# Expert blocks of a mixture of experts: token rows fetched by an indirect transfer and turned, in place of products with a matrix of zeros and ones

## The chip, the cores and the metric

The kernel runs on one core of one Trainium2 chip. The metric is the device time of one execution in microseconds (us), as the median over runs.

## What is computed

The program is three layers of a model on 512 tokens of width 1024, in float32: two layers of attention, convolution and pooling mixers with cross-attention and an MLP, and a third with four more mixers and a mixture of 32 experts, each token going to 4 of them. Only that last part, `moe_ffn`, is touched:

```python
logits = (xt @ router_w + router_b).astype(jnp.float32)
top_logits, top_idx = lax.top_k(logits, TOP_K)            # 4 of 32 experts
gates = jax.nn.softmax(top_logits, axis=-1)
...
def run_block(args):                                       # one block: up to 128 tokens of one expert
    tok, e = args
    hmid = xt[tok] @ w_gu[e] + b_gu[e]                     # xt[tok]: the gather
    glu = jnp.minimum(hmid[:, 0::2], SWIGLU_LIMIT)
    lin = jnp.clip(hmid[:, 1::2], -SWIGLU_LIMIT, SWIGLU_LIMIT)
    act = glu * jax.nn.sigmoid(SWIGLU_ALPHA * glu) * (lin + 1.0)
    return act @ w_down[e] + b_down[e]
```

`xt` is the RMS-normalised activation times a gain. The up product is 1024 x 2048, the down product 1024 x 1024.

## The kernel before

`out_norm_and_route` makes the last residual, normalises it tile by tile (128 tokens each), turns it for the router, and computes for every token and expert the place that the token has among the expert's tokens (`T.place`). It also keeps the normalised rows `T.y` as two float32r parts, `high` and `low` (`Parts.round` on ACT, L88, and `Parts.rest` on DVE, L91), 4 tiles of 128 tokens by 1024 features.

`first_blocks` then runs the 32 experts j = 0..31 in order, four to a turn of a hardware loop (experts 0 to 3 ahead of the loop, 28 to 31 behind it). Each expert's weights are 6 units of 2 MB (0 to 3 up, 4 and 5 down) in a ring of 6 slots of SBUF (`ring_view`). SP loads unit n of expert j+1 as soon as expert j is done with slot n, so the ring holds one expert.

An expert with at most 64 tokens is a half expert: `up_half`, `turn_act_half`, `down_half` use plain float32 products on 64 columns of the array, two at a time. One with more is a full expert. Its first unit is used in plain float32 (`up_parted`, L3829); for units 1 to 5, ACT rounds each quarter of the unit into the one buffer `moe_w_high` (L88), DVE takes the rest (L91), and `unit_products` makes three float32r products of each pair of quarter and half bank (L3799, L3800, L3804). DVE also makes the gated activation (`clip` L3856 and L3857, `multiply` L3863 and L3868) and splits its turned form (`split_act`, L3873). An expert ends with the bias products of the down part (L3820 full, L3660 half; those of the up part are L3820 and L3633).

The gather is two products. `make_sel` (DVE, L3513) writes for a pair of experts a matrix of zeros and ones, 512 tokens by 2 x 128 places; `gather` (PE, L3594 and L3595) multiplies the two parts of `T.y` by it. Every expert step of PE has two calls of it for the following pair, one between the up products and the turning of the activation, one between that turning (L3812, L3640) and the last down products; each call is 16 products of 256 columns. `save_gather` (DVE, L3530) multiplies the result by the gain into `T.xg`, which lies in the space of `hT`.

An expert with more than 128 tokens has its further tokens in an extra block; `extra_blocks` runs these behind the 32, here two, both half. They use the same `gather`, with nothing else around it. `combine_and_finish` fetches the 4 rows of each token with indirect transfers (POOL, L4578) and sums them.

Of the kernel before, what the change touches and what calls it, by code (L numbers as in the profile page):

```python
# [14 lines left out]
P = 128  # L15
# [90 lines left out]
class Core:  # L106


    def __init__(self, nc, ctx, ins, out):
# [15 lines left out]
        self.rows = nc.dram_tensor("expert_rows", [BLOCKS, P, D], F32, kind="Internal").ap()  # L125
        self.x_rows = nc.dram_tensor("x_rows", [P, TT, D], F32, kind="Internal").ap()
# [565 lines left out]
class TileNorm:  # L692

# [5 lines left out]
    def __init__(self, k, ctx, gain, dst, first=()):  # L701
        self.k = k
        self.tiles = list(first) + [(k.x[:, t, :], dst[:, :, t * P:(t + 1) * P], gain) for t in range(TT)]
        self.y = k.sb("tile_y", [P, 2, D], ctx=ctx)
        self.ss = k.sb("tile_ss", [P, len(self.tiles)], ctx=ctx)
        self.rms = k.sb("tile_rms", [P, len(self.tiles)], ctx=ctx)
        self.rstd = k.sb("tile_rstd", [P, len(self.tiles)], ctx=ctx)

    def square_and_root(self, act, t, added):
        k = self.k  # L710
        if added is not None:
            act.wait_ge(k.bank_free.sem, added)
        if t >= 2:
            act.wait_ge(k.turned.sem, k.turned.at(2 * t - 2))
        act.activation(self.y[:, t % 2, :], self.tiles[t][0], ACT.Square, accum_out=self.ss[:, t:t + 1])\
# [5 lines left out]
    def scale(self, dve, t):  # L721
        k = self.k
        dve.wait_ge(k.roots.sem, k.roots.at(t + 1))
        dve.reciprocal(self.rstd[:, t:t + 1], self.rms[:, t:t + 1]).then_inc(k.rstd.sem, 1)
        dve.wait_ge(k.rstd.sem, k.rstd.at(t + 1))
        dve.tensor_scalar(self.y[:, t % 2, :], self.tiles[t][0], self.rstd[:, t:t + 1], None, ALU.mult)\
           .then_inc(k.normalised.sem, 1)

    def turn(self, pe, t):
# [5 lines left out]
        for g in range(2):  # L735
            for c in range(4):
                f = 4 * g + c
                ins = pe.transpose(k.psum[:, self.TURNED + g, c * P:(c + 1) * P], self.y[:, t % 2, f * P:(f + 1) * P],
# [3 lines left out]
    def save_even(self, dve, t):  # L742
        k = self.k
        dve.wait_ge(k.turned.sem, k.turned.at(2 * t + 1))
        _, dst, gain = self.tiles[t]
        dve.tensor_tensor(dst[:, 0:4, :], k.psum[:, self.TURNED, :].rearrange("p (c s) -> p c s", c=4),
                          gain[:, 0:4].unsqueeze(2).broadcast_to([P, 4, P]), ALU.mult)\
           .then_inc(k.turned_even.sem, 1)

    def save_odd(self, act, t):  # L750
        k = self.k
        act.wait_ge(k.turned.sem, k.turned.at(2 * t + 2))
        _, dst, gain = self.tiles[t]
        for c in range(4):
            ins = act.activation(dst[:, 4 + c, :], k.psum[:, self.TURNED + 1, c * P:(c + 1) * P], ACT.Copy,
                                 scale=gain[:, 4 + c:5 + c])
        ins.then_inc(k.turned_odd.sem, 1)

    def passed(self):
        k = self.k  # L760
        for signal in (k.squares, k.roots, k.rstd, k.normalised, k.turned_even, k.turned_odd):
            signal.passed(len(self.tiles))
        k.turned.passed(2 * len(self.tiles))
# [2714 lines left out]
class Experts:  # L3478


    def __init__(self, k, name, tables, one_by_one):
# [7 lines left out]
        self.sel_ready = signal("sel_ready")  # L3489
        self.gathered = signal("gathered")  # L3490
# [15 lines left out]
    def make_sel(self, dve, r, blocks=2):  # L3506

        T = self.tables
        if not self.one_by_one and self.waits_from(r, 1):
            dve.wait_ge(self.gathered, 4 * r)  # L3510
        for h in range(blocks):
            for t in range(TT):
                ins = dve.tensor_scalar(T.sel[:, t, h, :], T.iota[:, :], T.place[:, t, bass.ds(blocks * r + h, 1)], None,  # L3513
                                        ALU.is_equal)
        ins.then_inc(self.sel_ready, 1)

# [6 lines left out]
    def save_gather(self, dve, n, half, par):  # L3523

        k, T = self.k, self.tables
        for b in range(2):
            dve.wait_ge(self.gathered, 2 * n + b + 1)
            f = 4 * half + 2 * b
            gain = T.gain[:, f:f + 2].unsqueeze(2).broadcast_to([P, 2, 2 * P])
            dve.tensor_tensor(T.xg[:, par, f:f + 2, :], k.psum[:, b, :].rearrange("p (f s) -> p f s", f=2),  # L3530
# [1123 lines left out]
```

## Time and profile before

| what | value |
|---|---|
| time, median of 3 runs | 3115.11 us (3108.37 to 3116.99) |
| time of the profiled execution | 3102.57 us |
| its span, first to last instruction | 3100.8 us |
| granted TensorE clock, mean over the span | 0.946 |
| PE busy | 2814.6 us, 91% |
| DVE busy | 1620.0 us, 52% |
| ACT busy | 1053.1 us, 34% |
| POOL busy | 154.8 us, 5% |
| HBM read and written | 581.73 MB and 41.16 MB |

The span is the time from the first to the last instruction. A clock of 1.00 is 2.4 GHz, 0.50 is 1.2 GHz. PE is TensorE's matmuls, PEld its weight loads, DVE VectorE, ACT ScalarE, POOL GpSimd, SP the engine that issues the weight loads from HBM. Busy times of matmuls are modelled and overlap, so distances between starts are used below and not sums of durations.

### The profile page before, as it was taken

The page shows a single profiled execution, that of the slowest core. Times are in us where ns is not written, and L with a number is a line of the kernel's source. Part 1 is how long each engine was busy: PE and PEld are TensorE (multiplying, and loading weights), DVE is VectorE, ACT ScalarE, POOL GpSimd, SP SyncE. Part 2 cuts the span into 40 slices and gives each one's busy share as a digit, 9 for nine tenths or more (in the row PEclk, how much of TensorE's full clock was granted, in tenths as well). Part 3 has the DMA queues.
Part 4 walks back from the last instruction along what each step waited for, and adds up shares of the span by engine and source line. Part 5 has one row for each costly group of instructions (what it writes and reads, how often), then busy time and mean ns, then how long its engine had stood idle before and what let it go on. Part 6 is the DMA issues. An engine that isn't in the chain of part 4 may idle for free. (4 is left out here: it accounts for less than half of the span.)

```text
span 3100.8 us, 36680 instructions
## 1 busy us (share of the span) xinstructions
PE 2814.6 (91%) x13802; PEld 2044.2 (66%) x13803; DVE 1620.0 (52%) x2423; ACT 1053.1 (34%) x1468; POOL 154.8 (5%) x171
## 2 busy tenths in 40 slices
PE   7877989999999899999966878999999999899982
PEld 6655768888878688888754665654766565466541
DVE  4864554444555544446855546652855454266413
ACT  4444443232224432233332241330634233144301
POOL 0530000000000000000012020000000000000002
PEclk9988999999999999999987788999999999999986
DMA  3110315444323132222210037999999899999994
GB/s 131 58 51 28 109 61 189 175 166 170 118 103 116 62 116 82 108 88 78 95 55 1 1 123 274 387 409 408 388 361 372 338 409 369 409 374 347 409 385 152
DMA packets 186386, 626.00 MB, mean 202 GB/s; under 512 B 9747, under 2 KB 15538, under 8 KB 185810
## 3 DMA queue, kind: packets, MB, share of 16 engines
q1 hardware_dynamic: 173328, 577.51, 49.1%
q10 hardware_dynamic: 10530, 37.02, 3.0%
q0 software_dynamic: 2304, 8.39, 0.7%
q8 instruction: 153, 2.51, 0.3%
q14 instruction: 71, 0.58, 0.1%
HBM read 581.73 MB, written 41.16 MB: 201 GB/s over the span
## 5 line engine op out<-in xcount | busy, mean ns | idle before, releaser
L91 DVE TENSOR_TENSOR unit_low<-unit_whole,unit_high 128x4096 fp32r<-128x4096 f32 (+3 forms) x95 | 287.3, 3029 | 177.4 <-ACT unit_high L88 165.5
L667 PE MATMUL psum<-tokens_high,unit_high 128*128 128x512 f32 (+2 forms) x1016 | 372.1, 366 | 4.4 <-PEq L873 1.6
L667 PE MATMUL psum<-tokens_high,unit_low 128*128 128x512 f32 (+2 forms) x1016 | 368.3, 363 | 0.0
L667 PE MATMUL psum<-tokens_low,unit_high 128*128 128x512 f32 (+2 forms) x1016 | 368.3, 362 | 0.0
L88 ACT ACTIVATE unit_high<-unit_whole 128x4096 fp32r<-128x4096 f32 (+2 forms) x65 | 225.8, 3474 | 377.1 <-PE psum L667 286.5
L88 ACT ACTIVATE moe_w_high<-ring_slot 128x1024 fp32r<-128x1024 f32 x208 | 215.9, 1056 | 60.0 <-PE psum L3804 59.1
L3627 PE MATMUL psum<-ring_slot,hT 128*64 128x512 f32 x1008 | 226.8, 599 | 7.5 <-DMA ring_slot<-in_moe_w_gu 7.5
L667 PEld LDWEIGHTS psum<-tokens_high,unit_high 128*128 128x128 f32 (+1 forms) x1016 | 190.9, 188 | 38.0 <-DVE unit_low L91 4.0
L667 PEld LDWEIGHTS psum<-tokens_low,unit_high 128*128 128x128 f32 (+1 forms) x1016 | 190.9, 188 | 31.6 <-issue 1.6
L667 PEld LDWEIGHTS psum<-tokens_high,unit_low 128*128 128x128 f32 (+1 forms) x1016 | 190.9, 188 | 30.6 <-issue 0.2
L667 PE MATMUL psum<-unit_high,hidden_high 128*128 128x512 f32 x512 | 199.5, 390 | 0.0
L667 PE MATMUL psum<-unit_high,hidden_low 128*128 128x512 f32 x512 | 199.2, 389 | 0.0
L667 PE MATMUL psum<-unit_low,hidden_high 128*128 128x512 f32 x512 | 199.2, 389 | 0.0
L3670 DVE TENSOR_SCALAR moe_glu<-psum 128x256 f32<-128x256 f32 x42 | 17.8, 425 | 330.9 <-PE psum L3633 239.8
L3627 PEld LDWEIGHTS psum<-ring_slot,hT 128*64 128x64 f32 x1008 | 76.8, 138 | 147.3 <-issue 146.2
L3594 PE MATMUL psum<-moe_sel,moe_y_high 128*128 128x256 f32 x576 | 151.9, 301 | 10.2 <-DVE moe_sel L3513 7.9
L1155 DVE TENSOR_TENSOR x_residual<-psum,x_residual 128x512 f32<-128x512 f32 x128 | 84.4, 687 | 117.7 <-PE psum L667 117.7
L3595 PE MATMUL psum<-moe_sel,moe_y_low 128*128 128x256 f32 x576 | 144.4, 288 | 0.0
L3799 PE MATMUL psum<-moe_w_high,moe_xg_high 128*128 128x512 f32 x312 | 131.1, 420 | 0.0
L91 DVE TENSOR_TENSOR unit_high<-ring_slot,moe_w_high 128x1024 fp32r<-128x1024 f32 x104 | 122.8, 1220 | 15.4 <-ACT moe_w_high L88 15.0
L3594 PEld LDWEIGHTS psum<-moe_sel,moe_y_high 128*128 128x128 f32 x576 | 113.3, 197 | 24.9 <-issue 14.2
L3684 ACT ACTIVATE moe_sig<-moe_glu 128x256 f32<-128x256 f32 x42 | 17.5, 417 | 313.5 <-DVE moe_glu L3670 313.4
(642 smaller groups left out, 5351.8 us busy)
## 6 DMA issues: line engine op xcount, KB each, us to landing
ring_slot<-in_moe_w_gu SPq DMA_DIRECT2D x102, 2048.0 KB, 16.0
unit_whole<-in_moe_w_gu SPq DMA_DIRECT2D x34, 2048.0 KB, 12.9
ring_slot<-in_moe_w_down SPq DMA_DIRECT2D x34, 2048.0 KB, 12.3
ring_last_slot<-in_moe_w_down SPq DMA_DIRECT2D x34, 2048.0 KB, 15.7
unit_whole<-in_w_up SPq DMA_DIRECT2D x16, 2048.0 KB, 8.4
unit_whole<-in_w_down SPq DMA_DIRECT2D x16, 2048.0 KB, 7.6
expert_rows<-zero_row ACTq DMA_DIRECT2D x15, 1536.0 KB, 5.3
unit_whole<-in_w_in SPq DMA_DIRECT2D x5, 2048.0 KB, 7.7
```

The source lines that it names most:

```text
L88: return act.activation(self.high, self.whole, ACT.Copy)
L91: return dve.tensor_tensor(self.low, self.whole, self.high.bitcast(F32), ALU.subtract)
L667: ins = pe.matmul(bank, a, c, start=(first and m == 0), stop=(last and m == len(parts) - 1))
L1155: dve.tensor_tensor(x, bank, x, ALU.add).then_inc(k.bank_free.sem, 1)
L3594: pe.matmul(bank, T.y.high[:, t, features], chosen, start=(t == 0), stop=False)
L3595: ins = pe.matmul(bank, T.y.low[:, t, features], chosen, start=False, stop=(t == TT - 1))
L3627: ins = pe.matmul(banks[g], xg[:, c, 0:HALF], w[c // HALF_K][:, c % HALF_K, g * 512:(g + 1) * 512], start=(c == 0), stop=False)
L3670: dve.tensor_scalar(T.glu[:, pair, :], bank[:, :, 0], 7.0, None, ALU.min).then_inc(self.glu_ready, 2)
L3684: act.activation(T.sig[:, pair, :], T.glu[:, pair, :], ACT.Sigmoid, scale=1.702).then_inc(self.gate_ready, 2)
L3799: pe.matmul(banks[g], a.high[:, f, :], w.high[:, cols], start=(first and q == 0), stop=False)
```

## The change

The normalised rows stay whole (`T.y`, float32) and are also stored to a table in HBM, `y_rows`, one DMA of 512 KB per tile, issued by ACT in place of the rounding. For every expert, `make_sel` writes the matrix of zeros and ones for this expert alone in bfloat16, and `find_tokens` multiplies it by a table `T.token` of two columns, which gives each place its token number (in two parts). `save_tokens` adds the parts up to an integer index; a place without a token gets an index beyond the table, which the transfer skips. `fetch_rows` is an indirect DMA by POOL of up to 128 rows of 4 KB into one of two buffers `T.y_of`; `turn_rows` turns them with 4 transposes per half, and `save_gather` applies the gain. The extra blocks still gather with a product, now in plain float32 on 128 columns.

```diff
-    def make_sel(self, dve, r, blocks=2):
+    def make_sel(self, dve, j, par):
+        if self.waits_from(j, 2):
+            dve.wait_ge(self.index_full, j - 1)
+        for t in range(TT):
+            ins = dve.tensor_scalar(T.sel[:, par, t, :], T.iota[:, :], T.place[:, t, bass.ds(j, 1)], None, ALU.is_equal)
         ins.then_inc(self.sel_ready, 1)
+    def find_tokens(self, pe, j, par):
+        pe.wait_ge(self.sel_ready, j + 1)
+        if self.waits_from(j, 2):
+            pe.wait_ge(self.xg_ready, 2 * (j - 1))
...
+        for t in range(TT):
+            ins = pe.matmul(k.psum[:, 1, 0:2], T.sel[:, par, t, :], T.token[:, t, :], start=(t == 0), stop=(t == TT - 1))
+        ins.then_inc(self.index_full, 1)
+    def save_tokens(self, dve, j):
+        dve.wait_ge(self.index_full, j + 1)
+        dve.tensor_scalar(T.index[:, bass.ds(j, 1)], k.psum[:, 1, 0:1], k.psum[:, 1, 1:2], float(S), ALU.add, ALU.add)\
+           .then_inc(self.index_ready, 1)
+    def fetch_rows(self, pool, j):
+        pool.wait_ge(self.index_ready, j + 1)
+        if j >= 2:
+            pool.wait_ge(self.gathered, 2 * (j - 2) + 2)
+        pool.indirect_dma_start(T.y_of[:, j % 2, :], None, k.y_rows, bass.IndirectOffsetOnAxis(ap=T.index[:, j:j + 1], axis=0),
+                                bounds_check=S - 1, oob_is_err=False).then_inc(self.fetched[j % 2], 16)
+    def turn_rows(self, pe, j, half, par, fetches=None, saved=None):
+        if half == 0:
+            pe.wait_ge(self.fetched[par], 16 * fetches)
...
+        else:
+            pe.wait_ge(self.index_ready, saved)
...
+        for f in range(4):
+            ins = pe.transpose(k.psum[:, half, f * P:(f + 1) * P], T.y_of[:, par, (4 * half + f) * P:(4 * half + f + 1) * P],
+                               k.ident[:, :])
+        ins.then_inc(self.gathered, 1)
...
# first_blocks, PE, one expert step
-                if ahead:
-                    E.gather(pe, pair + 1, j + 2, h, 0, saved=2 * (j + 1) + 1)
+                if following:
+                    if not (last and b == PER_ROUND - 2):
+                        E.find_tokens(pe, j + 2, par)
+                    E.turn_rows(pe, j + 1, 0, 1 - par, (PER_ROUND // 2) * i + (b + 1) // 2 + 1)
...
-                if ahead:
-                    E.gather(pe, pair + 1, j + 2, h, 1, saved=2 * (j + 1) + 2)
+                if following:
+                    E.turn_rows(pe, j + 1, 1, 1 - par, saved=j + 3 if not (last and b == PER_ROUND - 2) else EXPERTS)
# first_blocks, DVE, behind the activation of expert j
-                    E.save_gather(dve, j + 2, b % 2, 1 - b // 2)
+                        E.save_tokens(dve, j + 2)
+                    E.save_gather(dve, j + 1, 0, 1 - par)
+                    E.save_gather(dve, j + 1, 1, 1 - par)
# out_norm_and_route, ACT
-                    y_parts(t).round(act).then_inc(y_rounded, 1)
+                    act.dma_start(k.y_rows[t * P:(t + 1) * P, :], T.y[:, t, :]).then_inc(T.y_stored, 16)
```

TensorE in the step of a full expert, from its last down products of unit 4 on, before. `moe_act` is the activation that is turned, and its two parts are `moe_actT_high` and `moe_actT_low`:

```order
L3804 MATMUL psum<-moe_w_high,moe_actT_low 128x512 x2
L3812 MATMUL psum<-ident,moe_act 128x128 [waits first_act_ready]
L3812 MATMUL psum<-ident,moe_act 128x128 x3
L4145 UNCONDITIONAL_BRANCH
L3594 MATMUL psum<-moe_sel,moe_y_high 128x256 [waits first_xg_ready]
L3595 MATMUL psum<-moe_sel,moe_y_low 128x256
```

Fourteen more such products follow there. The same place of the changed kernel (`hT` holds the fetched rows):

```order
L3849 MATMUL psum<-ident,moe_act 128x128 [waits first_act_ready]
L3849 MATMUL psum<-ident,moe_act 128x128 x3
L4192 UNCONDITIONAL_BRANCH
L3556 MATMUL psum<-ident,hT 128x128 [waits first_xg_ready,first_index_ready]
L3556 MATMUL psum<-ident,hT 128x128 x3
```

Sixteen products give way to four transposes, and the wait is for `index_ready` of this step too. VectorE at the end of the same step, before:

```order
L91 TENSOR_TENSOR moe_last_low<-ring_last_slot,moe_w_high 128x1024 [waits unit_rounded] x4
L3873 TENSOR_TENSOR moe_actT_low<-psum,moe_actT_high 128x512 [waits first_actT_ready]
L4176 UNCONDITIONAL_BRANCH
L3530 TENSOR_TENSOR hT<-psum,feature_vectors 128x2x256 [waits first_gathered] x2
L3520 COPY moe_bias_ones<-moe_bias_pick 128x128
```

And in the changed kernel, where L3910 is the split of the turned activation that was L3873:

```order
L3910 TENSOR_TENSOR moe_actT_low<-psum,moe_actT_high 128x512 [waits first_actT_ready]
L4225 UNCONDITIONAL_BRANCH
L3532 TENSOR_SCALAR moe_index<-psum 128x1 [waits first_index_full]
L3571 TENSOR_TENSOR hT<-psum,feature_vectors 128x512 [waits first_gathered] x2
L3563 COPY moe_bias_ones<-moe_bias_pick 128x128
```

The write of the index, for which PE's second group of transposes waits, stands behind the split of the turned activation.

## Rows read from the trace of the kernel before

**Rows 1.** Windows: engines' busy us (instructions), granted clock, DMA share, GB/s.

```profile
1950.40:2971.80 1021.40, 986.66 (x4650) 587.34 (x4648) 519.95 (x777) 373.48 (x455) 0.00 (x0) 0.98 0.98 384
1950.40:2143.40 193.00, 187.45 (x918) 106.96 (x917) 93.94 (x172) 62.27 (x80) 0.00 (x0) 1.00 1.01 400
2605.80:2696.50 90.70, 81.82 (x415) 35.79 (x414) 17.36 (x52) 9.04 (x20) 0.00 (x0) 0.96 1.00 394
```

**Rows 2.** Groups of instructions, 1850 to 3101 us: busy us, mean ns, idle before.

```profile
L3594 PE MATMUL psum<-moe_sel,moe_y_high 128*128 128x256 f32 x576 | 151.9, 301 | 10.2 <-DVE moe_sel L3513 7.9 <-ACT moe_o L3704 2.3
```

**Rows 3.** Timeline of PE, expert 14 (full): start us, us, engine, line.

```profile
2353.50 7.13 PE L3829 MATMUL psum<-unit_whole,hT 128*128 128x512 f32 x16
...
2378.18 0.60 PE L3820 MATMUL psum<-moe_bias_parts,moe_bias_ones 128*128 128x512 bf16 x2
...
2380.52 0.39 PE L3799 MATMUL psum<-moe_w_high,moe_actT_high 128*128 128x512 f32 x1
...
2386.10 0.60 PE L3812 MATMUL psum<-ident,moe_act 128*128 128x128 f32 x4
2386.45 0.36 PE L3594 MATMUL psum<-moe_sel,moe_y_high 128*128 128x256 f32 x1
...
2388.41 0.40 PE L3799 MATMUL psum<-moe_w_high,moe_actT_high 128*128 128x512 f32 x1
...
2394.47 1.88 PE L3829 MATMUL psum<-unit_whole,hT 128*128 128x512 f32 x4
```

**Rows 4.** Timeline of PE, expert 30 (full, without gather products), idle before in brackets.

```profile
2924.54 0.60 PE L3820 MATMUL psum<-moe_bias_parts,moe_bias_ones 128*128 128x512 bf16 x2
...
2934.74 0.73 PE L3804 MATMUL psum<-moe_w_high,moe_actT_low 128*128 128x512 f32 x2 [1.18 <-DVE moe_actT_low L3873]
...
2940.06 1.51 PE L3627 MATMUL psum<-unit_whole,hT 128*64 128x512 f32 x6
```

**Rows 5.** Timeline of DVE, expert 30.

```profile
2929.47 4.62 DVE L91 TENSOR_TENSOR moe_last_low<-ring_last_slot,moe_w_high 128x1024 fp32r<-128x1024 f32 x4
2934.01 0.68 DVE L3873 TENSOR_TENSOR moe_actT_low<-psum,moe_actT_high 128x512 fp32r<-128x512 f32 x1
```

**Rows 6.** Timeline of PE, half experts: expert 13, then the second extra block.

```profile
2341.26 0.39 PE L3633 MATMUL psum<-moe_bias_parts,moe_bias_ones 128*64 128x512 bf16 x2
...
2343.80 0.66 PE L3640 MATMUL psum<-ident,moe_act 128*128 128x128 f32 x4
...
2346.27 3.65 PE L3655 MATMUL psum<-ring_slot,moe_actT 128*64 128x512 f32 x16
...
3035.43 0.41 PE L3633 MATMUL psum<-moe_bias_parts,moe_bias_ones 128*64 128x512 bf16 x2
3037.97 0.66 PE L3640 MATMUL psum<-ident,moe_act 128*128 128x128 f32 x4 [2.13 <-DVE moe_act L3677]
3039.38 5.04 PE L3655 MATMUL psum<-ring_slot,moe_actT 128*64 128x512 f32 x16 [0.75 <-ACT moe_actT L3695]
```

**Rows 7.** Waits and granted clock: PE's timeline at experts 7 and 12, three windows.

```profile
2120.86 4.51 PE L3627 MATMUL psum<-ring_slot,hT 128*64 128x512 f32 x20 [1.71 <-DMA ring_slot<-in_moe_w_gu]
2284.60 2.07 PE L3829 MATMUL psum<-unit_whole,hT 128*128 128x512 f32 x2 [3.28 <-issue]
...
2110.00:2125.00 15.00, 13.29 (x66) 4.71 (x64) 1.61 (x4) 1.60 (x3) 0.00 (x0) 1.00 1.03 410
2284.60:2327.30 42.70, 42.70 (x184) 31.00 (x184) 31.99 (x34) 24.18 (x26) 0.00 (x0) 0.96 0.93 359
3036.00:3044.00 8.00, 5.28 (x20) 1.98 (x22) 1.55 (x4) 1.07 (x3) 0.00 (x0) 0.79 0.00 0
```

**Rows 8.** PE's first up product; a fill and the last indirect transfers (POOL).

```profile
1887.56 2.80 PE L3627 MATMUL psum<-unit_whole,hT 128*64 128x512 f32 x12 [0.78 <-DVE hT L3530]
1794.11 1.80 POOL L4367 MEMSET moe_up_bias<- 128x2048 f32 x1 [45.49 <-POOLq L378]
ring_slot<-expert_rows,moe_row POOLq DMA_INDIRECT x12, 6.3
```

More of the change, by code:

```diff
@@ L125, in __init__ @@
         self.rows = nc.dram_tensor("expert_rows", [BLOCKS, P, D], F32, kind="Internal").ap()
+        self.y_rows = nc.dram_tensor("y_rows", [S, D], F32, kind="Internal").ap()
         self.x_rows = nc.dram_tensor("x_rows", [P, TT, D], F32, kind="Internal").ap()
@@ L689, in early_banks, with __init__ @@
         yield b
-class TileNorm:
+class RouterNorm:
     TURNED = 6
[L701 to L707, printed above, removed]
+    def __init__(self, k, ctx, gain, y):
+        self.k, self.gain, self.y = k, gain, y
+        self.ss = k.sb("tile_ss", [P, TT], ctx=ctx)
+        self.rms = k.sb("tile_rms", [P, TT], ctx=ctx)
+        self.rstd = k.sb("tile_rstd", [P, TT], ctx=ctx)
     def square_and_root(self, act, t, added):
         k = self.k
[L711 to L715, printed above, removed]
+        act.wait_ge(k.bank_free.sem, added)
+        act.activation(self.y[:, t, :], k.x[:, t, :], ACT.Square, accum_out=self.ss[:, t:t + 1])\
            .then_inc(k.squares.sem, 1)
@@ L3489, in __init__ @@
         self.sel_ready = signal("sel_ready")
+        self.index_full = signal("index_full")
+        self.index_ready = signal("index_ready")
+        self.fetched = [signal(f"rows_fetched{r}") for r in range(2)]
         self.gathered = signal("gathered")
@@ new lines, in make_extra_sel @@
+    def make_extra_sel(self, dve, b):
+        T = self.tables
+        for t in range(TT):
+            ins = dve.tensor_scalar(T.sel_whole[:, t, :], T.iota[:, :], T.place[:, t, bass.ds(b, 1)], None, ALU.is_equal)
+        ins.then_inc(self.sel_ready, 1)
+    def find_tokens(self, pe, j, par):
+        k, T = self.k, self.tables
+        pe.wait_ge(self.sel_ready, j + 1)
+        if self.waits_from(j, 2):
+            pe.wait_ge(self.xg_ready, 2 * (j - 1))
+        elif j == 1:
+            pe.wait_ge(self.index_ready, 1)
+        for t in range(TT):
+            ins = pe.matmul(k.psum[:, 1, 0:2], T.sel[:, par, t, :], T.token[:, t, :], start=(t == 0), stop=(t == TT - 1))
+        ins.then_inc(self.index_full, 1)
@@ L4123, in is_half, with _ @@
             return eng.value_load(T.count[0:1, bass.ds(j, 1)], min_val=0, max_val=S) < HALF + 1
+        @block.gpsimd
+        def _(pool):
+            pool.memset(T.y_of, 0.0).then_inc(k.pool_made.sem, 1)
+            pool.wait_ge(k.pool_made.sem, k.pool_made.at(1))
+            pool.wait_ge(T.y_stored, 16 * TT)
+            for j in range(EXPERTS):
+                E.fetch_rows(pool, j)
         @block.tensor
@@ L4168, in step @@
             def step(i, b, j, first, last):
+                par = b % 2
                 parted = not (first and b == 0)
-                xg = T.xg[:, b // 2, :, (b % 2) * P:(b % 2 + 1) * P]
+                xg = T.xg[:, par]
+                following = not (last and b == PER_ROUND - 1)
                 with dve.If(is_half(dve, j)):
```

188 lines of the change are left out of this document (90 added, 98 removed).

## The prediction

> **What bounds the kernel now.** I read the windows first. From the start of expert 2 to the end of expert 31 [rows 1] PE is busy 986.66 of 1021.40 us and the DMA engines have a share of 0.98 at 384 GB/s, with 400 and 394 GB/s in two stretches inside. So two resources are near their limit at once: where PE is freed, a transfer can take over. The other engines are at half. Next the groups [rows 2]: the first of the two gather products is 151.9 us busy in 576 instructions, and as many of the second follow them one by one. That is not what they cost, since matmuls overlap. So the timeline, at one full expert and one half.
>
> Expert 14, full [rows 3], takes 2353.50 to 2394.47 = 41.0 us and PE never waits. The first gather call lies between the up bias (2378.18) and the down products of unit 4 (2380.52): 2.34 us with the 0.26 us of the bias, so 2.08. The second lies between the transposes of the activation (2386.10) and unit 5 (2388.41): 2.31 us, of which 0.35 are the transposes, so 1.96. The gather costs 4.0 us per expert, 0.12 us per product.
>
> Now the last experts, which in the kernel before have no gather products at all, as there is no expert left to gather for. Expert 30 is full [rows 4]: from its up bias at 2924.54 to the next expert at 2940.06 it takes 15.52 us, where expert 14 takes 16.29 from the same bias. Four us of products are gone and 0.8 us is gained. The rest has turned into waits, and the rows say for whom: the product L3804 at 2934.74 waited for DVE L3873, the split of the turned activation, and DVE was busy without a pause ahead of it [rows 5]: four splits of unit 5 from 2929.47, then L3873 from 2934.01. From the up bias on, DVE needs 10.2 us until PE can go on (2934.74 - 2924.54), whatever PE does in the meantime. A full expert's gather is cover over DVE.
>
> The half expert tells the same [rows 6]. In expert 13 the transposes of the activation start 2.54 us behind the up bias (2341.26, 2343.80) with a gather call in between, and in an extra block, with nothing in between, also 2.54 us behind it (3035.43, 3037.97), PE idle for 2.13. The activation sets that time. Only the second distance shrinks: 2.47 us to the down products with a gather call (2343.80, 2346.27), 1.41 without (3037.97, 3039.38). So a half expert gains 1.06 us, not 4.0. And the down products behind this idle time took 5.04 us for 16, against 3.65 in expert 13: the granted clock of 3036 to 3044 is 0.79 [rows 7], between full speed and 0.5, where expert 13 ran at full speed.
>
> **The change, part by part.** *Half experts.* `find_tokens` and four transposes stand in the first gap and four transposes in the second. They are shorter than the idle time there: four transposes start 0.35 us apart as a group [rows 3], and the four products with two columns I put at 0.3 in all (bounds: nothing, and four of the 0.12 us of a gather product). So 2.13 becomes about 1.4 us of idle time and 0.75 about 0.45. Does the clock fall? At 2120.86 PE had been idle for 1.71 us and the clock stayed at 1.00 [rows 7]; behind 2.13 and 0.75 it fell. I take no fall, hence -1.06 us; with a fall it is +0.33 (5.04 - 3.65 = 1.39).
>
> *Full experts.* The second group of transposes waits for `index_ready` of this step (`saved=j+3`), because `find_tokens` has used the same PSUM bank; DVE writes that index only behind L3873, as the order shows. Queued behind this wait on PE are all products of unit 5. From the up bias: DVE's split is seen by PE at 10.2 us [rows 4]. The index is one more small DVE instruction, 0.2 (bounds 0.1 and 0.4): 10.4. Transposes 0.36: 10.76. Unit 5 and its bias, from 2388.41 to 2394.47 [rows 3], 6.06: 16.82. Before: 16.29. So **+0.53 us**, although 4.0 us of products are removed. `find_tokens` and the first transposes, ahead of unit 4, cost nothing as DVE covers them: without them PE would wait the longer. PE's idle time is then one piece: unit 4 ends near 6.5 us, the transposes of the activation near 7.1, the wait until 10.4: 3.3 us. Such a piece is in the trace. At the turns of the loop PE is idle 3.28 us, and expert 12 behind it takes 42.70 us at a mean clock of 0.96 [rows 7], where expert 14 took 41.0: the fall costs 1.7. I take it for every full expert: 0.53 + 1.7 = **+2.2 us**; expert 30, which gets transposes now, 16.82 + 1.7 - 15.52 = +3.0.
>
> For the transposes the Trainium skill has another price ("TensorE: Matmul & The Clock Gate", Part 4: PE-mode transpose): about 275 ns each in a kernel's context. The row says 0.35 us for four, in float32. By the page each full expert would be 0.75 us longer and the sum 10 us greater; the sum here goes by the row.
>
> *The transfers.* A fetch of expert j+1 is issued when its index is written, in the step of expert j-1, and needed behind the up products of expert j, over 20 us later even for two half experts. The last indirect transfers land 6.3 us after issue [rows 8]. Hidden. But they add bytes: 2048 rows of 4 KB at most, 8.4 MB or 64 rows per expert, 0.66 us each at the 400 GB/s of the busier stretch [rows 1]. Where PE waits for weights that counts in full, and there PE's gains and losses are swallowed.
>
> *The rest.* POOL's small fills and the table stand where POOL then waits for ACT. The stores of `y_rows` replace ACT's rounding, and DVE's four splits fall away, on a stretch in which PE's order of router and count products ends last; I count 0. At the start, two matrices, a product, the fill of `T.y_of` (1.80 us for 2048 columns [rows 8]) and a fetch of 6.3 us or more beside 4 MB of other loads stand in place of the gather; PE's first up product was at 1887.56 and I expect it within -2 and +4 us of that. I take 0. The Trainium skill has a lower price for such a fetch ("DMA: Bandwidth & Descriptors", Anatomy of one DMA — SWDGE (gpsimd) path: 2.0 us and the bytes at 436 GB/s, so 3.2 us for 512 KB). By it the start would be 3 us earlier, and the total by as much; the row is for the same kind of transfer and I stay with it. The gather of an extra block was 64 products of 0.12 us and becomes 32 in float32, which the trace counts as two each; with the 0.09 us of a float32 transpose per piece as the lower bound and 0.15 as the upper, -2 to +2 us each. I take 0.
>
> **The sum.** Of the experts 2 to 29, 12 are full and 16 half. Experts 2 to 8 (five half, two full) run at 400 GB/s and end on waits for weights, experts 21 to 23 (all half) at 394 [rows 1]. There only the bytes count: 10 x 0.66 = +6.6. Outside: 10 full x 2.2 = +22, 8 half x -1.06 = -8.5, expert 30 +3.0. Together **+23 us**. The profiled execution takes 3102.57 us, so 3126. It lies 12.5 below the median of the runs shown, 3115.11, to which the same step gives **3138**. A difference under 0.3%, 9 us, can't be told from none here.
>
> **The rivals.**
> *The half experts lose the clock too.* Their idle time shrinks only from 2.9 to about 1.9 us in two pieces, and the extra block shows the fall. Then the 8 outside the stretches that wait for weights pay 1.39 us each, and up to 8 inside them as well: 11 to 22 us more, 3149 to 3160. Chance 0.13.
> *The wait costs less than it seems, no change.* If the clock does not fall behind most of the waits of 3.3 us, as it did not behind 1.71, or the fall runs out before unit 5 starts, full experts come out at 0 to +0.5 and the sum at -1 to +5 (expert 30 at +1), 3114 to 3120. Chance 0.22.
> *Faster: what PE is freed of does come out.* This needs DVE's index in time: if the split of the turned activation is done when the transposes of the activation are, because PE hands on the rounding buffer earlier. Then a full expert saves 4.0 less 1.0 of new products and transposes and a half 1.06: -30 - 8.5 + 6.6 = -32, 3083. It decides from the point where DVE needs under 7 us from the up bias; it needed 9.5 until L3873 started in expert 30. Chance 0.11.
> *A fetch is late.* If the indirect transfers, beside loads that keep the engines full, take over 20 us, PE waits in every half step: if it is 25 us, 5 us in each of 16 half steps: +80, 3218. The 6.3 us of the last transfers [rows 8] speak against it, though fewer loads ran beside them. Chance 0.04.
> The forecast itself has 0.50.
>
> **How the numbers follow.** The forecast's own range, with the start (-2 to +4), the index (0.1 to 0.4 us each) and the extra blocks (4 us either way), is 3125 to 3150. Eight in ten must take in most of no change and of the slower case: 3105 to 3160. Faster by over 0.3% is the third rival and a tail of the second: 0.13. No change 0.22. Slower: 0.65.
>
> **What would show it.** In the changed trace, a full expert away from the loop's turn takes about 43 us, with one wait of some 3.3 us of the transposes L3556 for DVE's index L3532, and a granted clock of 0.5 in the products of unit 5. A half expert takes 25.1 us. The mean clock of the expert stage falls from 0.98 to about 0.93. Wrong would be: full experts of 38 us (DVE is no bound), clock at 1.00 behind the waits, or PE waiting for `rows_fetched`.

## The result and the profile after

The changed kernel takes 3120.11 us, median of 20 runs (3111.32 to 3130.64), the kernel before beside it 3109.60 us, median of 20 (3096.18 to 3120.75): a ratio of 1.0032, 95% interval 1.0020 to 1.0044. In a second measurement it was 3120.39 against 3107.06 us, 1.0051 (1.0037 to 1.0065). So the change costs 0.3 to 0.5% by the ratios, 10 to 16 us. Its profiled execution took 3119.28 us with a span of 3117.2 us and a mean granted clock of 0.936.

The windows of the changed kernel, with the columns of [rows 1]: from the start of expert 2 to the end of expert 31, then experts 2 to 8 and 21 to 23.

```profile
1948.50:2990.80 1042.30, 924.76 (x4060) 528.54 (x4097) 524.34 (x815) 371.71 (x455) 27.68 (x28) 0.97 0.98 384
1948.50:2180.40 231.90, 203.04 (x910) 104.85 (x914) 100.04 (x195) 63.44 (x84) 6.92 (x7) 0.96 1.01 400
2619.20:2709.10 89.90, 74.82 (x355) 29.34 (x354) 16.96 (x51) 9.02 (x20) 2.97 (x3) 0.94 1.01 397
```

Against [rows 1] PE has 62 us less to do in the experts (986.66 to 924.76), and they take 20.9 us longer (1021.40 to 1042.30). The groups of instructions from 1850 us on, as in [rows 2], say what PE waited for ahead of its new transposes (the number behind the last bar is the idle time, then its releasers):

```profile
L3556 PE MATMUL psum<-ident,hT 128*128 128x128 f32 x256 | 42.3, 291 | 51.3 <-DVE moe_index L3532 40.7 <-DMA hT<-y_rows,moe_index 10.4
```

151.9 us of products of one of two lines gave way to 42.3 us, and 40.7 us of waiting for the index came with them. The timeline of PE in expert 14, the expert of [rows 3], its start and then from the last bias product of the up part on:

```profile
2364.69 0.70 PE L3866 MATMUL psum<-unit_whole,hT 128*128 128x512 f32 x1
...
2389.29 0.38 PE L3857 MATMUL psum<-moe_bias_parts,moe_bias_ones 128*128 128x512 bf16 x1
2389.51 0.24 PE L3525 MATMUL psum<-moe_token,moe_sel 128*128 128x2 bf16 x4
2389.61 0.64 PE L3556 MATMUL psum<-ident,hT 128*128 128x128 f32 x4
2390.00 0.47 PE L3836 MATMUL psum<-moe_w_high,moe_actT_high 128*128 128x512 f32 x1
...
2395.68 0.60 PE L3849 MATMUL psum<-ident,moe_act 128*128 128x128 f32 x4
2399.64 0.66 PE L3556 MATMUL psum<-ident,hT 128*128 128x128 f32 x4 [3.36 <-DVE moe_index L3532]
2400.20 0.79 PE L3836 MATMUL psum<-moe_w_high,moe_actT_high 128*128 128x512 f32 x1
...
2403.72 0.40 PE L3836 MATMUL psum<-moe_w_high,moe_actT_high 128*128 128x512 f32 x1
...
2407.86 2.31 PE L3866 MATMUL psum<-unit_whole,hT 128*128 128x512 f32 x5
```

PE is idle for 3.36 us at the second group of transposes, and the products behind it are spaced 0.43 and not 0.23 us until 2403.6. From 2364.69 to 2407.86 the expert takes 43.2 us, where it took 41.0. The timeline of DVE there answers to [rows 5]:

```profile
2394.23 4.62 DVE L91 TENSOR_TENSOR moe_last_low<-ring_last_slot,moe_w_high 128x1024 fp32r<-128x1024 f32 x4
2398.77 0.69 DVE L3910 TENSOR_TENSOR moe_actT_low<-psum,moe_actT_high 128x512 fp32r<-128x512 f32 x1
2399.37 0.21 DVE L3532 TENSOR_SCALAR moe_index<-psum 128x1 f32 x1
```

The index stands behind five splits, and PE starts when it is written. Three windows, the wait, the 3.4 us behind it, and the same products in expert 10, with the clock as the third number from the end:

```profile
2396.30:2399.64 3.34, 0.00 (x1) 0.00 (x1) 3.34 (x6) 1.12 (x2) 0.00 (x0) 1.00 1.02 408
2400.20:2403.60 3.40, 3.40 (x9) 2.75 (x9) 1.68 (x6) 0.00 (x0) 0.99 (x1) 0.50 1.03 410
2258.60:2265.00 6.40, 6.33 (x29) 4.79 (x29) 2.06 (x7) 0.00 (x0) 0.99 (x1) 1.00 0.75 299
```

In expert 14 the granted clock is 0.50 for 3.4 us, in expert 10 it stays at 1.00 though its wait is as long. Expert 10 takes 41.6 us. The half expert 13, on PE (compare [rows 6]):

```profile
2353.26 0.39 PE L3670 MATMUL psum<-moe_bias_parts,moe_bias_ones 128*64 128x512 bf16 x2
2353.58 0.25 PE L3525 MATMUL psum<-moe_token,moe_sel 128*128 128x2 bf16 x4
2353.69 0.63 PE L3556 MATMUL psum<-ident,hT 128*128 128x128 f32 x4
2355.80 0.66 PE L3677 MATMUL psum<-ident,moe_act 128*128 128x128 f32 x4 [1.48 <-DVE moe_act L3714]
2356.30 0.61 PE L3556 MATMUL psum<-ident,hT 128*128 128x128 f32 x4
2357.46 3.65 PE L3692 MATMUL psum<-ring_slot,moe_actT 128*64 128x512 f32 x16 [0.55 <-ACT moe_actT L3732]
```

Idle for 1.48 and 0.55 us, forecast 1.4 and 0.45, and the down products take 3.65 us, so the clock stays. The only wait for a fetch is that of the first expert:

```profile
1886.35 1.97 PE L3556 MATMUL psum<-ident,hT 128*128 128x128 f32 x8 [10.38 <-DMA hT<-y_rows,moe_index]
1889.10 3.68 PE L3664 MATMUL psum<-unit_whole,hT 128*64 128x512 f32 x8 [0.78 <-DVE hT L3571]
```

The 32 fetches land 5.1 to 9.7 us after their issue, median 7.9. PE's first up product is at 1889.10 against 1887.56 [rows 8].

### The profile page after: what moved, and what is told of

Read it like the earlier page. It is cut to its first block and busy times, and to the rows that moved or that the text cites. A ratio compares the mean times of both kernels' runs of the same rounds, so it can differ in the third digit from the quotient of the medians.

```text
span 3117.2 us, 35590 instructions
## 1 busy us (share of the span) xinstructions
PE 2743.2 (88%) x13119; PEld 1974.0 (63%) x13163; DVE 1615.4 (52%) x2447; ACT 1047.2 (34%) x1464; POOL 190.6 (6%) x213
## 5 line engine op out<-in xcount | busy, mean ns | idle before, releaser
L668 PE MATMUL psum<-tokens_high,unit_high 128*128 128x512 f32 (+2 forms) x1016 | 372.2, 366 | 4.5 <-PEq L864 1.7
L668 PE MATMUL psum<-tokens_high,unit_low 128*128 128x512 f32 (+2 forms) x1016 | 368.4, 363 | 0.0
L668 PE MATMUL psum<-tokens_low,unit_high 128*128 128x512 f32 (+2 forms) x1016 | 368.3, 362 | 0.0
L88 ACT ACTIVATE unit_high<-unit_whole 128x4096 fp32r<-128x4096 f32 (+2 forms) x65 | 225.8, 3474 | 373.1 <-PE psum L668 282.3
L3664 PE MATMUL psum<-ring_slot,hT 128*64 128x512 f32 x1008 | 225.8, 596 | 11.7 <-DMA ring_slot<-in_moe_w_gu 11.7
L668 PEld LDWEIGHTS psum<-tokens_high,unit_high 128*128 128x128 f32 (+1 forms) x1016 | 190.8, 188 | 38.1 <-DVE unit_low L91 4.1
L668 PEld LDWEIGHTS psum<-tokens_low,unit_high 128*128 128x128 f32 (+1 forms) x1016 | 190.9, 188 | 31.6 <-issue 1.6
L668 PEld LDWEIGHTS psum<-tokens_high,unit_low 128*128 128x128 f32 (+1 forms) x1016 | 190.9, 188 | 30.7 <-issue 0.2
L668 PE MATMUL psum<-unit_high,hidden_high 128*128 128x512 f32 x512 | 199.5, 390 | 0.0
L668 PE MATMUL psum<-unit_high,hidden_low 128*128 128x512 f32 x512 | 199.2, 389 | 0.0
L668 PE MATMUL psum<-unit_low,hidden_high 128*128 128x512 f32 x512 | 199.2, 389 | 0.0
L3721 ACT ACTIVATE moe_sig<-moe_glu 128x256 f32<-128x256 f32 x42 | 17.5, 416 | 322.0 <-DVE moe_glu L3707 322.0
L91 DVE TENSOR_TENSOR unit_low<-ring_slot,moe_w_high 128x1024 fp32r<-128x1024 f32 x104 | 121.2, 1217 | 0.0
L1136 DVE SCALAR_TENSOR_TENSOR hT<-psum,hidden_relu 128x512 f32<-128x512 f32 x64 | 43.8, 689 | 147.3 <-ACT hidden_relu L1108 147.3
L668 PEld LDWEIGHTS psum<-unit_high,hidden_low 128*128 128x128 f32 x512 | 96.1, 188 | 19.9
## 6 DMA issues: line engine op xcount, KB each, us to landing
ring_last_slot<-in_moe_w_down SPq DMA_DIRECT2D x34, 2048.0 KB, 17.1
```

Of the source, the lines that this page charges most:

```text
L88: return act.activation(self.high, self.whole, ACT.Copy)
L91: return dve.tensor_tensor(self.low, self.whole, self.high.bitcast(F32), ALU.subtract)
L668: ins = pe.matmul(bank, a, c, start=(first and m == 0), stop=(last and m == len(parts) - 1))
L1136: dve.scalar_tensor_tensor(out=hidden[j % 2].whole[:, b, :], in0=bank, scalar=0.0, in1=relu[:, h % 2, :], op0=ALU.max, op1=ALU.mult)\
L3664: ins = pe.matmul(banks[g], xg[:, c, 0:HALF], w[c // HALF_K][:, c % HALF_K, g * 512:(g + 1) * 512], start=(c == 0), stop=False)
L3721: act.activation(T.sig[:, pair, :], T.glu[:, pair, :], ACT.Sigmoid, scale=1.702).then_inc(self.gate_ready, 2)
```

## The experiments

Each ratio is against the kernel before, run on the same chip in the same measurement, with its 95% interval. A full expert is said to be away from the turns if it does not follow a turn of the hardware loop (that is, not 12, 20 or 24) and does not end at one (15).

**The index written early.** `save_tokens` is moved ahead of the splits of unit 5 in full experts. In half ones it stands where it stood, behind the activation.

```diff
             multiply(pair)
+            if pair == 1 and tokens:
+                self.save_tokens(dve, j + 2)
             for q in range(HALF_K):
                 self.split_quarter(dve, j, n + 1, q)
```

> The changed kernel, but DVE writes the token index of expert j+2 right behind the second product of the gated activation of a full expert, ahead of the splits of unit 5, and not behind the split of the turned activation. Theory A (the loss is the wait for an index queued late on DVE, and the clock that falls behind it): the waits of 3.36 us before L3556 are gone, the 12 full experts with a full set of transposes take about 40.6 us (expert 30 of the kernel before took 40.2) and not 43.2, the clock stays at 1.00 in them, and the time is about 30 us under the changed kernel, some 20 under the one before: ratio to before 0.993 to 0.996. Theory B (the fetch's bytes and the waits for weights set the time): nothing is gained over the changed kernel, ratio 1.002 to 1.004.

Measured: 3099.10 us, 0.9982 (0.9971 to 0.9994), less of a gain than expected. PE in expert 14 of this kernel (its first product is at 2358.0):

```profile
2389.44 0.60 PE L3556 MATMUL psum<-ident,hT 128*128 128x128 f32 x4
2390.96 0.49 PE L3836 MATMUL psum<-moe_w_high,moe_actT_high 128*128 128x512 f32 x1 [0.92 <-ACT moe_actT_high L3945]
...
2392.96 0.73 PE L3841 MATMUL psum<-moe_w_high,moe_actT_low 128*128 128x512 f32 x2 [0.82 <-DVE moe_actT_low L3910]
...
2398.13 1.45 PE L3866 MATMUL psum<-unit_whole,hT 128*128 128x512 f32 x3
```

One wait of 3.36 us has become two of 0.92 and 0.82 us, and the expert takes 40.1 us. So the place of one DVE instruction of 0.22 us is what turned a small gain into a loss. The two waits that are left are of the kind that expert 30 had before [rows 4]. In experts 2, 5, 9 and 18 the clock fell behind them and these took 41.8 to 42.4 us. Much of the rest of the expected gain is missing where PE waits for weights: in this one trace experts 2 to 8 take 228.4 us and 21 to 23 take 92.3, where the kernel before has 222.5 and 89.4 in the mean of three.

**Few gather products, nothing else.** The kernel before, with 2 of the 16 products in each gather call of the expert steps, so that the experts compute on wrong rows. Nothing is fetched.

```diff
-            for t in range(TT):
+            for t in range(tiles):
...
+                if tiles == TT:
+                    pe.matmul(bank, T.y.high[:, t, features], chosen, start=(t == 0), stop=False)
...
-                    E.gather(pe, pair + 1, j + 2, h, 0, saved=2 * (j + 1) + 1)
+                    E.gather(pe, pair + 1, j + 2, h, 0, saved=2 * (j + 1) + 1, tiles=1)
```

> The kernel before, but each gather call of an expert step makes 2 of its 16 products (one token tile, one part), so the experts compute on a part of the tokens. It shows what the removed products were worth: summed by their distance, 14 x 2 x 0.12 = 3.3 us per expert, 105 us in all, if PE's time counted in full: ratio 0.966. Theory A (they cover DVE and ACT): full experts 40.3 us as expert 30, half experts 25.1 us, or 26.5 and more where the clock falls behind the idle time of 1.9 us: -8 to -25 us, ratio 0.992 to 0.998.

Measured: 3106.05 us, 1.0000 (0.9991 to 1.0010), where 0.992 to 0.998 was expected. Seven eighths of the gather's products, some 3.5 us per expert, are gone, and the time is the same. Full experts away from the turns take 40.1 to 40.2 us where the clock stays and 41.5 to 41.9 where it falls, which it does in 6 of 8. The clock also falls in half experts, in 7 of the 8 that lie outside the stretches that wait for weights. Expert 13 takes 28.4 us, where it took 26.2:

```profile
2341.47 0.66 PE L3641 MATMUL psum<-ident,moe_act 128*128 128x128 f32 x4 [1.72 <-DVE moe_act L3678]
2343.12 6.62 PE L3656 MATMUL psum<-ring_slot,moe_actT 128*64 128x512 f32 x16 [0.68 <-ACT moe_actT L3696]
```

PE is idle for 1.72 and 0.68 us here, and in the changed kernel for 1.48 and 0.55, where expert 13 kept the clock in all three executions. So the gather was cover, as the prediction had it, and its removal alone is worth nothing: the 0.9 to 1.0 us that an expert gains where the clock stays go into the falls and into longer idle times at the turns of the loop (4.6 to 4.8 us where 3.2 to 3.4 us were before).

**No rows moved.** Every index lies beyond the table, so the indirect transfer skips all rows. The experts compute on zeros.

```diff
-        dve.tensor_scalar(T.index[:, bass.ds(j, 1)], k.psum[:, 1, 0:1], k.psum[:, 1, 1:2], float(S), ALU.add, ALU.add)\
+        dve.tensor_scalar(T.index[:, bass.ds(j, 1)], k.psum[:, 1, 0:1], k.psum[:, 1, 1:2], float(2 * S), ALU.add, ALU.add)\
```

> The changed kernel, but each index lies beyond the table, so the 32 transfers are issued and move no row; the experts compute on zeros. It takes 8.4 MB of transfers away and nothing else. Prediction's term: the bytes count 0.66 us per expert where PE waits for weights, 10 experts, so about -7 us against the changed kernel, ratio to before 1.001, with experts 2 to 8 shorter by 5 us and 9 to 20 unchanged. If bytes don't matter at all: ratio 1.003. If the fetch costs the weight loads more than its bytes (their landing time went from 16 to 18 us), over 10 us less: ratio below 1.000.

Measured: 3114.87 us, 1.0031 (1.0019 to 1.0043). In the trace experts 2 to 8 take 224.7 us, against 231.9, 228.8 and 231.5 in three executions of the changed kernel. That looks like 6 us for the rows, but the kernel called Both below moves them and takes 224.7 us there too, and the other variants of the changed kernel that move them take 225.8 to 228.6. So a cost of the rows is not shown. In the whole time the ratio was expected at 1.001 and is that of the changed kernel, 1.0032 and 1.0051, within the uncertainty.

**The wait filled with 13 products.** float32r products of 512 columns into a free bank, behind the transposes of the activation in full experts.

```diff
         self.turn_act_pair(pe, j, 1)
+        x = self.tables.xg_parts.high
+        for n in range(FILLERS):
+            pe.matmul(self.k.psum[:, 4, :], x[:, 0, :], x[:, 0:4, :].rearrange("p f s -> p (f s)"), start=True, stop=True)
```

> The changed kernel with 13 products of 512 float32r columns (3.0 us) put on PE behind the transposes of the activation of a full expert, into a bank that is free there; nobody reads them. The wait for the index stays, only it is filled. Theory A (a wait of 3.3 us costs 1.7 us more by the fall of the clock): full experts take 41.6 us and not 43.2 where the clock fell, the 0.5 level is no longer seen in unit 5, and the time is 12 to 16 us under the changed kernel: ratio to before 0.998 to 1.000. Rival (the fall lies in time that DVE would make PE wait for anyway): full experts stay at 43 us, ratio 1.003.

Measured: 3130.95 us, 1.0090 (1.0072 to 1.0108), slower than the changed kernel, where 0.998 to 1.000 was expected. The eight full experts away from the turns do what was expected, 41.6 to 42.5 us at a clock of 1.00. But PE's idle time at the loop's turns, 3.28 us in [rows 7], has grown:

```profile
2295.03 2.92 PE L3866 MATMUL psum<-unit_whole,hT 128*128 128x512 f32 x3 [9.54 <-issue]
```

Three such turns cost 6.2 us more each, 19 us together.

**The same number of products, 16 columns each.** Their work is gone and their number stays.

> The kernel with 13 filling products in the wait of the full experts, with 16 columns each in place of 512: as many instructions at the same place, but little work. PE's idle time at the loop's turns (experts 11 to 12, 19 to 20, 23 to 24) was 3.3 us without fillers, 9.5 us with 13 of 512 columns, and 3.4 us followed by a second one of 0.7 to 1.9 us with three. If it is the number of instructions in the loop's body that counts, it is 9.5 us again here. If it is what PE did ahead of the turn (work that keeps it from running ahead of its instructions), it is 3.3 us. In the full experts the wait for the index stays above 2 us in either case and the clock falls behind it in most of them, so that they take 43 us.

One execution, 3143.19 us, with 3110.84 us for the kernel before beside it. The turn is still long, so the work of the filling products is not what lengthens it. What is left is that they are there, 52 instructions more in a turn of the loop:

```profile
2303.49 2.92 PE L3866 MATMUL psum<-unit_whole,hT 128*128 128x512 f32 x3 [9.23 <-issue]
```

The wait for the index is 2.0 us here, and the full experts away from the turns take 42.8 to 43.6 us with the clock fallen, but for expert 10 with 41.7.

**Three products in the wait.** Plain float32, 0.89 us each.

```diff
         self.turn_act_pair(pe, j, 1)
+        for n in range(3):
+            pe.matmul(self.k.psum[:, 4, :], xg[:, 0, :], xg[:, 0:4, :].rearrange("p f s -> p (f s)"), start=True, stop=True)
```

> The changed kernel with three plain float32 products of 512 columns (0.89 us each, 2.7 us) in the wait of 3.36 us of every full expert, in place of the 13 float32r products of the earlier kernel, so that the code of a loop turn grows by 12 products and not by 52. If the idle time of 9.5 us at the loop's turns came from the length of the code, it is back at 3.3 us here; the clock then stays at 1.00 in the full experts, these take 41.7 us, the 9 falls of 1.6 us are gone (-14 us in the profile, span 3102 to 3106) and the ratio to the kernel before is 0.998 to 1.000. If something else in the filler lengthened the turn (its place in the code), the turns stay at 9.5 us and the ratio is 1.006 to 1.009. If the falls cost less without the profiler than with it, the turns are 3.3 us and the ratio is 1.001 to 1.003.

Measured: 3113.53 us, 1.0026 (1.0014 to 1.0037), where the changed kernel had 1.0051 in the same measurement: 7 us less by the medians, half of what was expected. The eight full experts away from the turns all take 41.6 to 41.8 us, and none has a fall. At the turns the idle time is 3.38 us again, but in experts 12, 20 and 24 a second one follows:

```profile
2289.65 2.41 PE L3866 MATMUL psum<-unit_whole,hT 128*128 128x512 f32 x5 [3.38 <-issue]
2293.96 4.54 PE L3866 MATMUL psum<-unit_whole,hT 128*128 128x512 f32 x6 [1.90 <-issue]
```

**Both.** The index early, and one float32 product of 0.89 us ahead of unit 4's down products.

> The changed kernel with the index written early (as in the earlier kernel, which measured 0.9982 of the kernel before) and one plain float32 product of 512 columns, 0.89 us, ahead of the down products of unit 4 of a full expert, where PE otherwise waits 0.92 us for DVE. It adds no time if it ends within that wait. If the two waits of 0.92 and 0.82 us together are what let the clock fall in 5 of the full experts (1.7 us each), one of them alone does not: full experts 40.1 us at a clock of 1.00, 5 falls gone, -6 to -9 us, ratio 0.995 to 0.997. If the falls come from elsewhere, the ratio stays at 0.998.

Measured: 3097.46 us, 0.9973 (0.9961 to 0.9984), faster than both kernels: 9.6 us by the medians below the one before, at the upper end of the 0.995 to 0.997 that was expected. All eight full experts away from the turns take 40.2 to 40.9 us at a clock of 1.00. PE in expert 14, where one wait is left:

```profile
2386.30 0.60 PE L3556 MATMUL psum<-ident,hT 128*128 128x128 f32 x4
2387.82 0.49 PE L3836 MATMUL psum<-moe_w_high,moe_actT_high 128*128 128x512 f32 x1 [0.92 <-ACT moe_actT_high L3946]
```

The expectation had the place of the waits wrong. PE does not wait ahead of unit 4; the wait of 0.92 us stands ahead of unit 5, for ACT, and is still there. The added product puts unit 4 and all behind it 0.9 us later, and so the second wait, 0.82 us for the split of the turned activation, is used up.

The falls of experts 2, 5, 9 and 18 are gone, and one each in 12 and 24, 9 us together. Against the index alone only 3 us are seen in the ratio, and the two intervals overlap, so that these two kernels are not told apart. In the profile two falls came back elsewhere, in the half experts 16 and 19 (27.0 and 30.9 us, there 25.3 and 28.8), and experts 21 to 23, which wait for weights, took 93.9 us against 92.3.

**Both kernels again.** Each twice more, nothing altered.

> The changed kernel once more, nothing altered, for two questions. Does the granted clock fall behind the same waits? In its first profile it fell in 9 of the 12 full experts from 2 to 27 that have the wait of 3.36 us, and each fall cost 1.6 us. If a fall behind this wait is a matter of phase, other experts are spared this time, the total is 8 to 11 of 12, and the span lies within 5 us of 3117.2. If it is fixed by the work, experts 10, 15 and 18 are spared again. The rival is that the profile of the changed kernel was an unlucky one: then 4 to 6 fall now and the span is 3107 to 3111. Time against the kernel before: 1.002 to 1.004.

> The kernel before once more, one look, for how far two profiled executions of one kernel differ. The first had a span of 3100.8 us with no fall of the granted clock in a full expert away from the loop's turn. If such falls are a matter of phase only where PE is idle, there are none again, a full expert is 41.0 us again, and the span differs by less than 4 us, the difference lying in the stretches that wait for weights. If the first profile was a lucky one by the 12.5 us that it lay below the shown median, the span is 3108 to 3114 now.

> The changed kernel a third time. From the start of expert 2 to the end of expert 31 the two executions so far took 1042.3 and 1036.0 us, with the granted clock falling in 9 of 12 full experts in both, and in the same ones. I expect 1034 to 1044 us and 8 to 10 falls; experts 10, 15 and 18 are spared if it is fixed by what lies ahead of them.

> The kernel before a third time. From the start of expert 2 to the end of expert 31 the two executions so far took 1022.5 and 1022.3 us, while the unchanged code ahead of the experts ended up to 8 us apart. I expect 1021 to 1025 us for the experts, and no fall of the granted clock in a full expert away from the loop's turns.

The windows from the start of expert 2 to the end of 31, first the second and third execution of the changed kernel, then of the one before:

```profile
1948.30:2984.30 1036.00, 926.29 (x4099) 527.17 (x4097) 524.70 (x815) 371.89 (x455) 27.78 (x28) 0.97 0.98 385
1947.90:2992.20 1044.30, 930.44 (x4099) 531.59 (x4097) 523.99 (x815) 371.60 (x455) 27.69 (x28) 0.96 0.98 383
```

```profile
1958.00:2980.30 1022.30, 985.98 (x4651) 586.81 (x4649) 520.91 (x781) 373.48 (x455) 0.00 (x0) 0.98 0.99 384
1955.00:2972.40 1017.40, 980.51 (x4650) 586.01 (x4648) 520.70 (x781) 373.51 (x455) 0.00 (x0) 0.99 0.98 384
```

The spans were 3110.2 and 3119.5 us for the changed kernel, 3108.8 and 3101.7 for the one before. That is wider apart than expected: the second execution of the kernel before has a span 8.0 us above its first, where under 4 was expected, and its third takes 1017.4 us for the experts, where 1021 to 1025 was expected. The falls behind the wait are not fixed by the work: 9 of the 12 full experts from 2 to 27 in the first two executions, the same nine, and 12 of 12 in the third, where 8 to 10 were expected. Expert 10 in the third has the same wait as before and is spared no longer (0.63 us a product instead of 0.39):

```profile
2257.38 1.12 PE L3556 MATMUL psum<-ident,hT 128*128 128x128 f32 x4 [3.36 <-DVE moe_index L3532]
2258.15 0.78 PE L3836 MATMUL psum<-moe_w_high,moe_actT_high 128*128 128x512 f32 x1
2258.72 0.63 PE L3837 MATMUL psum<-moe_last_low,moe_actT_high 128*128 128x512 f32 x1
```

## Why the prediction was right in direction and too large in size

The mechanism was right and the sum too large: +23 us was forecast, the medians say +10.5 and +13.3. 3120.11 us lies below the forecast's own range of 3125 to 3150, at the end of what the second rival gave (3114 to 3120). Two steps failed. The fall of the clock was taken for every full expert and the wait for expert 30 too, +25 us where +17.5 was measured. And the time ahead of the experts was put at nothing, where three executions of each kernel have the changed one 6.6 us earlier. Two other terms erred the other way, experts 2 to 8 by 3.7 us and the half experts by 3.4, and hid most of the first error; that the sum of the experts came within 4.5 us is partly luck.

The mean of three executions of each kernel, split as the prediction splits it. The parts are distances between starts on PE; "start" runs from the router products at 1846.59 us of the kernel before (1845.04 after), with little changed ahead of it, to expert 2.

| term | predicted, us | measured, us |
|---|---|---|
| start | 0 | +0.3 |
| experts 2 to 8 | +4.6 | +8.3 |
| experts 21 to 23 | +2.0 | +0.1 |
| 10 full experts outside | +22 | +17.1 |
| 8 half experts outside | -8.5 | -5.1 |
| expert 30 | +3.0 | +0.5 |
| expert 31, to the first extra block | 0 | -1.5 |
| extra blocks and the rest | 0 | -1.1 |
| sum | +23 | +18.5 |
| the code ahead of the router products | 0 | -6.6 |
| span | +23 | +11.9 |

*The mechanism of the full expert.* Right in each step: the index seen 10.35 us behind the bias products (2389.29 to 2399.64; forecast 10.4), a wait of 3.36 us (forecast 3.3), 41.6 us without a fall (forecast +0.53, measured +0.6) and 43.2 us with one (forecast +2.2, measured +2.2).

*The step that failed on the full experts* is "I take it for every full expert", said of the fall's 1.7 us. Of the ten outside the stretches that wait for weights, seven, seven and ten had the fall. Expert 15 gained or lost nothing in any execution, as it ends at a turn of the loop where PE had waited 2.8 to 3.2 us already: its loss went into that idle time, which is 0.6 to 2.0 us now. +22 was +15.4, +17.4 and +18.4.

*Expert 30* was sized at +3.0 with the wait for the index and a fall. No `find_tokens` is left in its step, so its second transposes wait for an index that had long been written. PE waits 0.76 and 0.96 us there, where it waited 1.20 and 1.18, and the clock fell in one execution of three. This was to be read from the diff (`else EXPERTS`).

*The half experts.* Five of the eight outside gained 0.8 to 1.0 us each, near the forecast of 1.06, with the clock at 1.00 in all but one of the 24 cases in the three executions. But experts 17 and 29 gave it back in waits for weights (0.86 and 2.86 us of PE idle in the first execution, ahead of the second half of their up products), and took 0.4 and 1.4 us longer in the mean; the stretches that wait for weights do not end at expert 8. Expert 16 gained 2.6, as its clock no longer falls behind the shorter idle time at the turn.

*The bytes.* 0.66 us per expert is not shown. Over 2 to 8 the loss was +8.3 where +4.6 was forecast, in 21 to 23 it was +0.1 for +2.0. The kernel without rows takes 6 us less than the changed one over 2 to 8, but so does the one called Both, which moves them.

*The clock of the stage* was forecast to fall from 0.98 to about 0.93 and came to 0.97, 0.97 and 0.96. The forecast's own numbers give no more: 13 falls that cost 1.7 us each are 22 us of 1040, which takes 0.02 from the mean and not 0.05.

*Between the sum and the medians.* The profiled executions confirm most of the sum: +18.5 of +23. What is left lies ahead of the changed region. In three executions of the kernel before, the router products started at 1846.6, 1854.1 and 1851.1 us, in three of the changed one at 1845.0, 1842.8 and 1844.2. The two kernels' code is the same up to the normalisation just ahead of that point, and 4.7 of the 6.6 us are there long before it: one product of code that both share (L667, in the changed kernel L668) starts at 1088.5, 1092.8 and 1089.7 us in the kernel before, and at 1084.7, 1085.4 and 1086.7 us in the changed one. The prediction had no term for it. The spans, +11.9 us, agree with the medians, +10.5 and +13.3. Whether those 6.6 us are chance or come from where the shorter program puts its code was not tested: the kernel before with few gather products, which is shorter too, was at 1844.8, and the six variants of the changed kernel at 1844.4 to 1849.6. It stays open.

*The level.* 3138 rested on the 3115.11 us of three runs; 20 and 23 runs gave 3109.60 and 3107.06. Of the 18 us by which 3138 is above 3120.11, 5.5 are this, 4.5 the sum, and the remaining 8 what lies between sum and medians.

*The rivals.* That the half experts lose the clock happened once in those 24 cases (expert 29 of the second execution). It was nearer than that: with few gather products and PE idle for 1.7 us and then 0.4 to 0.9, where the changed kernel has 1.4 to 1.5 and then 0.3 to 0.7, it happened in 7 of 8. That what PE is freed of comes out faster needed the index early, and the kernel that writes it early is faster, 0.9982; by the rule given for it, DVE would have had to be done under 7 us from the bias products. It was still at 10, and the gain is smaller for that. No fetch was late but the first. Partly the no-change rival came true: some falls did not come.

*The prices.* Four float32 transposes start 0.39 us apart as a group (2389.61 to 2390.00). The Trainium skill ("TensorE: Matmul & The Clock Gate", Part 4: PE-mode transpose) has about 275 ns each, for bfloat16 in one kernel's context; for a group of four in float32 back to back this trace does not agree. The duration column, 0.60 to 0.66 us for four, overlaps the next product. The fetch of 512 KB at most landed after 7.9 us in the median. The estimate of 3.2 us from the figures of the Trainium skill ("DMA: Bandwidth & Descriptors", Anatomy of one DMA — SWDGE (gpsimd) path) was too low beside the weight loads; the row of 6.3 us was nearer.

## What to carry to other kernels

Freeing the busiest engine is worth nothing where its work covers another engine's: look for a place where the trace already runs without that work (here the expert with nothing left to gather), and read what the waits there are. A new small instruction whose result is waited for belongs ahead of the long ones in its engine's order: moving one of 0.22 us was worth 0.5 to 0.7%. And a wait's price is its length plus the fall of the clock behind it, which comes in some executions and not in others; count it with a share, and take the level of the kernel before from more than three runs.

## What was not expected of the hardware

PE's idle time at a turn of the hardware loop changes with the program's instructions and not with their work. Ahead of experts 12, 20 and 24 it was 3.2 to 3.4 us in both kernels, 9.2 to 9.6 us with 13 more products in the full branch of each of the four steps, whether of 512 or (one execution) of 16 columns, and 3.3 to 3.4 us followed by 0.7 to 1.9 us with three more. With fewer it is not shorter, though: 4.6 to 4.8 us in the kernel with few gather products. Ahead of expert 16, behind a full expert, it was 2.8 to 3.2 us before and 0.6 to 2.0 us in the changed kernel. What sets it was not settled.

The granted clock fell behind an idle time of 3.4 us in 9, 9 and 12 of 12 cases of the same kernel. In the full experts away from the turns it fell behind 2.0 us in 7 of 8 (the 16-column products), behind 0.76 to 0.92 and 0.82 to 1.02 us with four products between them in 4 of 8 (the index early), and never in 16 cases behind a single wait of 0.76 to 0.92 us (the kernels with three products and with both changes). In the half experts outside it fell behind 1.4 to 1.5 and then 0.3 to 0.7 us in 1 of 24, and behind 1.7 and then 0.4 to 0.9 us in 7 of 8. But in expert 30 of the kernel before it stayed behind 1.20 and 1.18 to 1.20 us in 3 of 3. A fall lasts 3.4 us at 0.50 and costs 1.6 us in a full expert. In two of the 30 falls of the changed kernel behind the index, both in its third execution, it lasted 6.8 us, and expert 10 took 44.0 us with that.
